# Expert-choice kernel: gather in fp32 from x, a fifth expert unit loaded aside, router scores by token tiles, and a split final norm

## The reference, cut to what matters

```
aff = softmax(einsum('bsd,de->bse', x, router_w), axis=-1)
gates, idx = top_k(aff.transpose(0, 2, 1), 32)
xg = x[idx]                                              # 16 experts x 32 tokens x 1024
hid = silu(xg @ w1[e]) * (xg @ w3[e])                    # 1024 x 1024 each
ye = (hid @ w2[e]) * gates[..., None]
out = zeros.at[idx].add(ye)
```

## Time and profile before

| what | value |
|---|---|
| median of 3 runs | 2186.15 us (2185.86 to 2186.26) |
| the profiled execution's own time | 2185.28 us |
| its span, first to last instruction | 2183.3 us |
| mean granted TensorE clock | 0.962 |
| busy: PE, DVE, ACT, POOL | 1911.9, 1059.3, 712.3, 75.6 us |
| HBM read | 621.76 MB, 285 GB/s over the span |

### The profile page before, as it was taken

How to read it: one execution, slowest core, us unless ns; L and a number is a source line. 1 busy time by engine, 2 the same in 40 slices (tenths; PEclk the granted TensorE clock), 3 DMA queues, 4 the chain that set the end, 5 groups by cost and what they waited for, 6 DMA issues and landing times. The chain is left out here.

```text
span 2183.3 us, 32580 instructions
## 1 busy us (share of the span) xinstructions
PE 1911.9 (88%) x13124; PEld 1354.3 (62%) x13140; DVE 1059.3 (49%) x1607; ACT 712.3 (33%) x1096; POOL 75.6 (3%) x137
## 2 busy tenths in 40 slices
PE   9999667676788986676768999999999999999998
PEld 6765224232366542242324888988888888888887
DVE  4761002010077500020103877787777877787776
ACT  5532002020046210020102433565444433565442
POOL 0000000000010000000000000000000000000000
PEclk9999989998999998898999999999999999999999
DMA  7399999999982899999999655436564655446550
GB/s 243 139 381 427 428 428 423 429 424 427 421 343 72 353 426 430 427 424 428 424 428 398 226 177 205 139 136 212 178 206 155 212 174 201 146 136 207 180 201 19
DMA packets 187952, 624.05 MB, mean 286 GB/s; under 512 B 17655, under 2 KB 129369, under 8 KB 163033
## 3 DMA queue, kind: packets, MB, share of 16 engines
q1 hardware_dynamic: 187864, 622.84, 73.6%
HBM read 621.76 MB, written 1.05 MB: 285 GB/s over the span
## 5 line engine op out<-in xcount | busy, mean ns | idle before, releaser
L3028 PE MATMUL psum<-x_both,up_hi 128*128 128x512 f32 x1408 | 352.9, 393 | 2.5 <-DVE x_both L525 2.2
L2275 PE MATMUL psum<-weight_ring,arena 128*32 128x256 f32 x3840 | 249.5, 411 | 106.7 <-DMA weight_ring<-in_w 106.1
L3028 PEld LDWEIGHTS psum<-x_both,up_hi 128*128 128x128 f32 x1408 | 257.4, 188 | 57.4 <-issue 3.3
L2275 PEld LDWEIGHTS psum<-weight_ring,arena 128*32 128x32 f32 x3840 | 123.5, 116 | 233.8 <-DMA weight_ring<-in_w 133.5
L2415 DVE TENSOR_TENSOR arena<-arena,psum 128x256 f32<-128x256 f32 x32 | 13.5, 421 | 450.6 <-PE psum L2275 450.6
L2297 PE MATMUL psum<-weight_ring,arena 128*32 128x512 f32 x1024 | 148.0, 709 | 73.6 <-DMA weight_ring<-in_w 63.6
L3080 DVE TENSOR_TENSOR up_lo<-weight_ring,up_hi 128x2048 fp32r<-128x2048 f32 x84 | 192.1, 2287 | 13.0 <-ACT up_hi L3051 12.8
L3031 PEld LDWEIGHTS psum<-x_both,up_lo 128*128 128x128 f32 x1408 | 189.4, 188 | 13.5
L3031 PE MATMUL psum<-x_both,up_lo 128*128 128x256 f32 x1408 | 193.2, 280 | 0.0
L3092 DVE TENSOR_REDUCE arena<-psum 128x256 f32<-128x512 f32 x176 | 121.5, 690 | 125.3 <-PE psum L3031 124.2
L652 PE MATMUL psum<-w_lo,x_both 128*128 128x384 f32 (+3 forms) x768 | 170.2, 359 | 2.4 <-DVE mix_lo L793 1.2
(11 more groups left out here) (390 smaller groups left out, 2393.7 us busy)
## 6 DMA issues: line engine op xcount, KB each, us to landing
weight_ring<-in_w SPq DMA_DIRECT2D x184, 2048.0 KB, 25.7
weight_ring<-in_ffn_wg SPq DMA_DIRECT2D x44, 1024.0 KB, 6.0
weight_ring<-in_ffn_wu SPq DMA_DIRECT2D x44, 1024.0 KB, 8.6
weight_ring<-in_ffn_wd SPq DMA_DIRECT2D x44, 1024.0 KB, 5.0
weight_ring<-in_w_in SPq DMA_DIRECT2D x14, 1536.0 KB, 6.7
weight_ring<-in_w_o SPq DMA_DIRECT2D x4, 2048.0 KB, 16.2
arena<-in_w SPq DMA_DIRECT2D x4, 2048.0 KB, 14.9
weight_ring<-in_ple_gate_w SPq DMA_DIRECT2D x4, 2048.0 KB, 25.0
```

The source lines that it names most:

```text
L2275: last = pe.matmul(ps[j * CAP:(j + 1) * CAP, 4 + k // 2, 0:QW], tokens[:, cc, :], w[c][:, j * QW:(j + 1) * QW], start=cc == 0, stop=cc == ...
L3028: last = pe.matmul(ps[:, 4 + 2 * f + h, :], w_part[:, f, h, c, :], x_both[:, :, c, :], start=c == 0, stop=False, skip_group_check=True)
```

## The change

`ASIDE` becomes 5: the first half of w2 of expert 1 is loaded aside too, in `x_cols` and `ln_params`. To free these, x is no longer split into rows_hi and rows_lo. `gather_first` and `gather` multiply x itself in plain fp32, with its chunks read with a step of 8 words, as fp32 stationary operand. The repeats of the one-hot columns in `gather_first` go from 4 (256 columns) to 2 (128 columns).

The order of the ring changes: expert 0's first unit is unit 12, the ple table 13, expert 0's next four are 14 to 17, expert 1's last unit is 18 and expert 0's last unit 19, and expert 2 has 20 to 25. `place_of` maps the old numbering to this. `issue_early` loads unit 19 once ple is used up, unit 18 once expert 0's first unit is, then units 20 to 23, and then waits until `used` has reached `early[1] + 6` = 20, that is until expert 1's last unit is used up, before unit 24. The memset of line 1756 gives one of its two counts earlier, after the peaks of heads 6 and 7. The first aside unit is issued in `mix_out_norm` right behind p (whose place in the arena moves), the new fifth one in two halves after the output projection and after the last tile of x, the load of the ring's later units behind it.

The router part is done by token tiles: only two of the four ple products stand ahead of it, each tile of x is turned, split and multiplied in its own 24 products of 128 tokens, and the other two ple products take the place of 20 idle ones while DVE selects. Several semaphores get shared names, with no other effect. `final_norm` takes a root per tile, scales in halves (three on DVE, one on ACT) and stores four halves. The diff, cut to its core:

```diff
-FIRST, ASIDE = 2, 4
+FIRST, ASIDE, SPARE_PART = 2, 5, 3
...
-        for e in range(EXPERTS):
-            for part in parts[ASIDE if e == 1 else 0:]:
+        stream.add(parts[0], 0)
+        stream.add(ple_projection, layer)
+        for part in parts[1:5]:
+            stream.add(part, 0)
+        stream.add(parts[5], 1)
+        stream.add(parts[5], 0)
+        for e in range(FIRST, EXPERTS):
+            for part in parts:
                 stream.add(part, e)
             if e in GATE_BEHIND:
...
-        0, 4096, 8192, 10240, 12544, 14688, 15712, 14336)
+        9216, 4096, 8192, 10240, 12544, 14688, 15712, 14336)
...
+            sp.dma_start(Arena(0).take(SLOT), stream.aside[layer][0]).then_inc(signal("aside_unit_0_arrived").sem, 16)
...
+            dve.memset(stat[:, 24:25], 0.0).then_inc(stream.used, 1)
...
-            dve.memset(stat[:, 24:25], 0.0).then_inc(stream.used, 2)
+            dve.memset(stat[:, 24:25], 0.0).then_inc(stream.used, 1)
...
+                        [x_cols.rearrange("p c q -> p (c q)"), ln_params.rearrange("p k n -> p (k n)")]]
...
+        def keep_tile_high(act, a):
+            for half in range(2):
+                act.wait_ge(tile_turned.sem, tile_turned.at(2 * a + half + 1))
+                act.copy(tile_columns(gate_hi, a, half), tile_bank(a, half)).then_inc(tile_high.sem, 2)
+        def keep_tile_low(dve, a):
+            for half in range(2):
+                dve.wait_ge(tile_high.sem, tile_high.at(2 * (2 * a + half + 1)))
+                dve.tensor_tensor(tile_columns(gate_lo, a, half), tile_bank(a, half),
+                                  tile_columns(gate_hi, a, half).bitcast(F32), ALU.subtract).then_inc(columns_made.sem, 2)
+        def logit_products(pe, a):
+            passes = ((router_hi, gate_hi), (router_hi, gate_lo), (router_lo, gate_hi))
+            for c in range(DC):
+                if c % (DC // 2) == 0:
+                    pe.wait_ge(columns_made.sem, columns_made.at(2 * (2 * a + c // (DC // 2) + 1)))
+                for k, (w_part, x_part) in enumerate(passes):
+                    last = pe.matmul(ps[0:EXPERTS, LOGIT_BANK, a * P:(a + 1) * P], w_part[:, c, :],
+                                     x_part[:, c, a * P:(a + 1) * P], start=c == 0 and k == 0,
+                                     stop=c == DC - 1 and k == len(passes) - 1)
+            if a == TILES - 1:
+                last.then_inc(logit_rows.sem, 1)
         def load(sp):
...
+        @block.tensor
+        def _(pe):
+            ple_products(pe, (0, 1))
+            pe.wait_ge(summed_rows.sem, summed_rows.at(0))
+            idle_products(pe, 6, 3)
+            turn_tile(pe, 0)
+            idle_products(pe, 6, 3)
+            turn_tile(pe, 1)
+            pe.wait_ge(router_low_kept.sem, router_low_kept.at(1))
+            for a in range(TILES):
+                logit_products(pe, a)
+        @block.scalar
+        def _(act):
+            act.wait_ge(routers_loaded.sem, 16 * DEPTH)
+            act.wait_ge(mixed.sem, mixed.at(0))
+            act.copy(router_hi[:, :, :], router).then_inc(router_high.sem, 1)
+            keep_ple(act, 0), keep_ple(act, 1)
+            keep_tile_high(act, 0), keep_tile_high(act, 1)
+        @block.vector
+        def _(dve):
+            keep_tile_low(dve, 0), keep_tile_low(dve, 1)
+        close_columns()
...
+        swapped = {early[0]: ple_unit, early[0] + 5: early[0] + 6, early[1] + 5: early[0] + 5}
+        place_of = lambda u: swapped.get(u, u)
+        def issue_early(sp):
+            sp.wait_ge(stream.used, ple_unit + 1)
+            stream.load(sp, early[0] + 6, 0)
+            sp.wait_ge(stream.used, ple_unit + 2)
+            stream.load(sp, early[0] + 5, 1)
+            stream.issued = early[0] + 7
+            stream.issue(sp, third + 4)
+            sp.wait_ge(stream.used, early[1] + 6)
...
-        REPEATS = BANK // 2 // (FIRST * CAP)
-        first_chunks = ps[:, FIRST_BANK:FIRST_BANK + 4, :].rearrange("p b (d u s) -> p (b d) u s", d=2, u=REPEATS)
+        REPEATS = 2
...
         def gather_first(pe):
-            for part in (rows_hi, rows_lo):
-                for a in range(TILES):
-                    for c in range(DC):
-                        if part is rows_lo and c % (DC // 2) == 0:
-                            pe.wait_ge(rows_low.sem, rows_low.at(2 * a + c // (DC // 2) + 1))
-                        last = pe.matmul(first_chunks[:, c], part[:, a, c * P:(c + 1) * P],
-                                         one_hot[:, a, 0:FIRST * CAP].rearrange("p (u s) -> p u s", u=1)
-                                         .broadcast_to([P, REPEATS, FIRST * CAP]),
-                                         start=part is rows_hi and a == 0 and c % 2 == 0,
-                                         stop=part is rows_lo and a == TILES - 1, skip_group_check=True)
+            for a in range(TILES):
+                for c in range(DC):
+                    last = pe.matmul(first_chunks[:, c, 0:REPEATS], in_chunks(x[:, a, :])[:, :, c],
+                                     one_hot[:, a, 0:FIRST * CAP].bitcast(F32).rearrange("p (u s) -> p u s", u=1)
+                                     .broadcast_to([P, REPEATS, FIRST * CAP]),
+                                     start=a == 0 and c % 2 == 0, stop=a == TILES - 1, skip_group_check=True)
             last.then_inc(gathered.sem, 1)
         def gather(pe, chunks):
...
                 if c >= 4:
                     pe.wait_ge(kept.sem, kept.at(c - 3))
                 for a in range(TILES):
-                    for part in (rows_hi, rows_lo):
-                        last = pe.matmul(ps[:, c % 4, :], part[:, a, c * P:(c + 1) * P], one_hot[:, a, :],
-                                         start=a == 0 and part is rows_hi,
-                                         stop=a == TILES - 1 and part is rows_lo)
+                    last = pe.matmul(ps[:, c % 4, :], in_chunks(x[:, a, :])[:, :, c], one_hot[:, a, :].bitcast(F32),
+                                     start=a == 0, stop=a == TILES - 1)
...
+            stream.issue(sp, early[0] + 5)
+            sp.wait_ge(mixed.sem, mixed.at(0))
+            load_aside(sp, 4, 0)
             tile_ready(sp, 1)
-            for k, (src, parts, arrived) in enumerate(zip(stream.aside[layer], aside_places[0:ASIDE - 1], aside_arrived)):
...
+            load_aside(sp, 1, 0)
+            load_aside(sp, 4, 1)
+            sp.wait_ge(logit_rows.sem, logit_rows.at(1))
+            load_aside(sp, 2, 0), load_aside(sp, 2, 1)
+            issue_early(sp)
...
-            idle_products(pe, 20)
+            ple_products(pe, (2, 3))
+            idle_products(pe, 2, 0)
...
-            down(pe, early[1], arrived_early, at[1])
+            down(pe, early[1], arrived_early, at[1], aside=ASIDE)
...
+            for s, n, (a, h) in ((vector_done, 1, (0, 0)), (vector_done, 2, (0, 1)), (scalar_done, 1, (1, 0)),
+                                 (vector_done, 3, (1, 1))):
+                sp.wait_ge(s.sem, s.at(n))
+                sp.dma_start(out[0, a * P:(a + 1) * P, h * BANK:(h + 1) * BANK], half(normed, a, h)
+                             ).then_inc(stored.sem, 16)
+            sp.wait_ge(stored.sem, 16 * 2 * TILES)
...
+            act.wait_ge(gains.sem, gains.at(2))
+            act.wait_ge(rooted.sem, rooted.at(2))
+            act.activation(half(normed, 1, 0), gained, ACT.Copy, scale=roots[:, 1:2]).then_inc(scalar_done.sem, 1)
...
+                root = roots[:, a:a + 1]
+                pool.wait_ge(squared.sem, squared.at(2 * a + 2))
+                pool_chain.link(pool, pool.tensor_scalar(root, half_sums[:, a, 0:1], half_sums[:, a, 1:2], EPS * D,
+                                                         ALU.add, ALU.add))
+                pool.tensor_tensor(root, root, half_power[:, 0:1], ALU.pow).then_inc(rooted.sem, 1)
...
+            half_ready(dve, 1, 1)
+            dve.tensor_tensor(gained, half(x, 1, 0), half(ln_params, 0, 0), ALU.mult).then_inc(gains.sem, 1)
+            for a, h in by_vector:
+                dve.wait_ge(rooted.sem, rooted.at(a + 1))
+                dve.scalar_tensor_tensor(out=half(normed, a, h), in0=half(x, a, h), scalar=roots[:, a:a + 1],
+                                         in1=half(ln_params, 0, h), op0=ALU.mult, op1=ALU.mult
+                                         ).then_inc(vector_done.sem, 1)
```

More of the change, by code:

```diff
@@ L2187, in before_columns, with tile_bank @@
[L2187 to L2194 removed]
+        tile_turned, tile_high = signal("columns_turned"), signal("columns_high_kept")
+        LOGIT_BANK = 5
+        def tile_bank(a, half):
+            return ps[:, 2 * a + half, :].rearrange("p (c q) -> p c q", c=DC // 2)
@@ L2292, in down @@
                     more_zeros(pe, zeros)
-                w = stream.slot(slot_unit + 4 + k).rearrange("p (r h n) -> p r h n", r=4, h=2)
-                pe.wait_ge(stream.arrived[(slot_unit + 4 + k) % WEIGHT_SLOTS], arrival(slot_unit + 4 + k))
+                if 4 + k < aside:
```

(26 more changed lines are left out.)

119 lines of the change are left out of this document (51 added, 68 removed).

## The result

The changed kernel took 2196.84 us (median of 5 runs, 2194.79 to 2198.78), the kernel before 2186.26 (also 5 runs). The ratio is given as 1.0053, with a 95% interval of 1.0042 to 1.0063; the quotient of the two medians is 1.0048. The profiled execution took 2195.73 us, 10.45 more than the one of before. I had written 2192.0 and a range of 2188 to 2208: slower, as forecast, but by nearly twice as much.

A forecast was written before the change was run, and what follows sets the result against it. The expert layers were taken as bound by DMA, any idle paid in full. 2 x (4.1 - 0.2) - 1.9 = +5.9 us on 2185.28 gave 2191.2, plus 0.87 for the median: 2192.0 us, range 2188 to 2208.

The forecast's parts named there:

- the race: Between the first release and expert 1's last: 24.5 us of DMA against a PE stretch of 28.91 us, PE losing.
- gather in plain fp32: Six chunks of gather on PE between the releases: 1.72 us a chunk instead of 0.96, +4.6 us in all.
- The price of the race: Expert 1's last release comes 33.5 us after the first, the 16 units after 29.4: +4.1 us a layer.
- `gather` covers either load: In gather, 0.43 us an instruction hides the weight load at either estimate of its cost.
- gather_first, the term that was mis-sized: Before the first release: 4.7 us with strided loads instead of 4.04, +0.7 a layer, upper end +5.4.
- the sign of being wrong: For gather_first: over 8 us would show the forecast wrong, 4 to 5 us right.
- the strided stationary operand is slow: Rival, chance 0.10: each 128-column load of gather_first takes 0.29 us instead of 0.147, +4.7 a layer, 2201.4 us.
- Router by tiles: Router products before the first release: 128-column products at 0.058 us end at about 140.1, -0.9 us a layer.
- narrow products cost like plain fp32: Rival, chance 0.22: 128-column fp32r router products cost as plain fp32, 7.4 us more in each layer, 2206.8 us.
- First release: PE chain up to the first ring slot's release: -0.9 + 0.7 = -0.2 us a layer, from -1.8 to +11.9.
- Tail: Final norm: scaling after the last root takes about 0.7 us instead of 2.6, -1.9 us, from -0.6 to -2.5.
- The other side: Rival, chance 0.09: between the releases the fp32 chunk is cheap and the DMA lead pays, 2182.8 or 2174 us.

The follow-up runs named there:

- The zeros: The kernel before with 24 products of zeros, 5.5 us, on PE ahead of expert 1's down products in both layers: 2190.2 us, ratio 1.0021.
- the other order of loads: The changed kernel with expert 2's last unit loaded once expert 0's last is used up, ahead of the wait for expert 1's last: 2190.54 us, ratio 1.0016.
- the kernel with rows apart: The changed kernel with w1 and w3 holding every 128th row (step 1, pieces of 4,096 bytes) and expert 2's last unit loaded first: 2208.53 us, ratio 1.0103.

## Why the prediction was right, and where its terms were off

**The bound and the race, right.** I predicted that PE would lose the race between the releases, and the 33.5 us between them. It was 33.86 us in both layers. The step "gather in plain fp32" used 0.86 us a product; measured were 7.15/16 = 0.447 us an instruction, two to a product, so 0.89. The price of the race, +4.1 a layer, came out as +4.0 and +4.8. The zeros and the fp32 gather in the old kernel confirm the mechanism from the other side, and the other order of loads gives back 2.7 and 3.5 us of it. The fall of the DMA share is there too, but at 185 to 195 us and not at 181 to 190, partly because the first release came 2.6 us late. I had also said that `gather` covers either load. It does, but for 0.4 us a layer: its 32 instructions took 14.8 us with a step of 8 and 14.4 with a step of 1 (the kernel with rows apart).

**gather_first, the term that was mis-sized.** I took +0.7 and gave 5.4 as the upper end; it was +3.9 a layer (7.91 less 4.04). The step that failed is to take 0.073 us, a group's busy time over its count, for the price of one load of 64 columns with a step of 4, and to double it to 0.147 for 128 columns. That going from 4 to 8 need not cost more holds: 329 and 335 ns. But one load of 128 columns takes 0.247 us of PE's time. The trace of before had the warning, in the mean duration of the loads themselves. The second row is of a contiguous operand of 64 columns; the one that I compared with (L3329) is a single value repeated, and takes 137 ns:

```profile
L2285 PEld LDWEIGHTS psum<-ident,arena 128*64 128x64 f32 x512 | 34.0, 214 | 34.2 <-issue 34.2
L1252 PEld LDWEIGHTS psum<-weight_ring,arena 128*64 128x64 f32 x32 | 1.9, 136 | 1.3 <-issue 0.5 <-ACT weight_ring L1240 0.2
```

The step of 4 cost 78 ns more for 64 columns. Twice that on top of the 192 ns of 128 contiguous columns gives 348 as an estimate, near the 335 measured. Busy time over count hid it, because these loads overlap one another: 214 ns each, 34.0 us for 512. Why they overlap more than those of `gather_first` is open.

With 7.9 us the step stayed just under the sign of being wrong that I had set, 8 us, and well outside the 4 to 5 that I had named as right. The rival "the strided stationary operand is slow" had put 0.29 on it and 2201.4 on the kernel; I had given it 0.10. So this is mostly that rival's mechanism on top of my forecast. The time of 2196.8 lies between the two numbers, just above the forecast's own range (2188 to 2196); only the room left for the rivals covers it. With +3.9 in place of +0.7 my sum would have been 2192.0 + 6.4 = 2198.4.

The SBUF — State Buffer page of the Trainium skill, in its specifications, says that two hits on each 16-byte line are needed for full bandwidth. The loads agree, at the exact place: steps of 1 and 2 words have two or more hits a line and took 192 and 196 ns, steps of 4 and 8 have one and took 329 and 335. The free step of 4 fp32, which the prediction took from the same page's note on cachelines, doesn't hold here: a step of 4 cost the load 137 ns more than a step of 1.

**Router by tiles, right in kind.** Products of 128 columns stand 0.06 us apart (136.81 to 139.69), so their cost goes with the columns, and the rival "narrow products cost like plain fp32", at 0.22 the largest, is refuted. The scores are copied at 139.95 instead of 141.21: -1.3, where I took -0.9.

**First release.** -1.3 + 3.9 = +2.6 in layer 0, as measured, instead of -0.2.

**Tail.** -1.07 in the trace, -1.0 alone, where I took -1.9. I had counted scaling only, and that part came as forecast: from the last root to the end of scaling it is 0.82 us (2189.99 to 2190.81) where it was 2.59. But with a root per tile the last root ends 5.58 us behind the start of the additions, where it was 4.83, so 0.75 of the gain goes there.

**The sum.** 2 x (4.1 - 0.2) - 1.9 was +5.9. By the rows it is 6.6 + 7.0 - 1.1 = 12.5, of which 10.6 arrived in the span. Most of the missing 1.9 goes between 60 MB and the last unit of layer 0. PE got that unit at 594.66 before and at 599.71 after, 5.05 late and not 6.6. The kernels with 2.5 to 3.9 us of delay at 60 MB gave up 1.2 to 1.6 there as well. It isn't the transfers that catch up, for the bytes are still 6.2 us late at 240 MB (637.6 against 631.4 us). What takes it up I didn't settle.

**The other side** would have needed a chunk to cost 0.27 us or less over the old one; it was 0.8. The DMA never got the lead that the fifth unit could have given.

## What to carry to other kernels

When a load-bound stage has a ring, look at which release stands at the head of the DMA queue and race PE's stretch to it against the bytes that can still move; a wait on a later release can undo a whole unit of lead. Before an operand of TensorE is read in place with a step, price the weight load at that step by itself, from the mean duration of a load and not from a group's busy time over its count; it can set the pace of a narrow product. And a data layout that mends the step should be checked for the size of the DMA pieces, over the whole stream and not only where it was mended.

## What the runs showed of the hardware that was not expected

- A weight load of 128 fp32 columns took 192 ns with a step of 1, 196 with 2, 329 with 4 and 335 with 8. There is a jump between 2 and 4, and next to nothing on either side of it; 3 was not run.
- The rate of full DMA engines fell with the piece: 426 to 428 GB/s with 16,384 bytes, 421 to 424 with 8,192 and 414 to 415 with 4,096. The share of busy time was 1.01 or 1.02 in all three, so the share alone doesn't show it. The shorter pieces of a partition also lay apart in memory; no run tells the two apart.
- In layer 0 the granted clock fell to the 1.2 GHz level in the middle of `gather_first`, behind 0.8 us of bf16 zeros and in the midst of slow loads; in layer 1, with the same instructions, it stayed at 2.4 GHz. The windows of the changed kernel in both layers, and then layer 1's step in PE's timeline, 7.90 us where layer 0 had 7.91:

```profile
149.50:152.50 3.00, 3.00 (x14) 3.00 (x14) 0.77 (x3) 0.00 (x0) 0.00 (x0) 0.51 0.97 410
738.00:741.00 3.00, 3.00 (x14) 3.00 (x14) 0.57 (x2) 0.00 (x0) 0.00 (x0) 1.00 1.04 442
```

```profile
736.76 7.90 PE L2504 MATMUL psum<-one_hot,x 128*128 128x128 f32 x32
```

  Where the load set the pace, half the clock cost nothing here.
- One unlucky stretch of clock is worth more than a microsecond in a single profile. The last `down` of layer 0 took 3.24 us before and 3.32 in the first trace after, but 1.92 in the second trace of the same changed kernel. Windows over its middle in those three traces, in that order, have the granted clock at the 1.2 GHz level twice and then at 2.4. Differences of a microsecond between two single traces should be read with that in mind.

```profile
596.00:598.00 2.00, 1.91 (x12) 0.17 (x4) 0.04 (x1) 0.05 (x1) 0.00 (x0) 0.50 1.06 391
601.00:603.10 2.10, 2.03 (x12) 0.22 (x4) 0.02 (x1) 0.02 (x1) 0.00 (x0) 0.50 1.03 384
599.60:601.70 2.10, 1.92 (x16) 0.42 (x16) 0.00 (x0) 0.00 (x0) 0.00 (x0) 1.00 1.02 398
```
